# One gain row spread over the partitions by VectorE, and the normed rows of four tiles kept transposed in DRAM, in a hybrid decoder block on eight cores

## The reference, cut to what matters

```python
h = rms_norm(x, norm_mix_g)                  # the normed rows; norm_mix_g is "g1" below
proj = h @ w_in                              # (B, S, 5888)
a_b, a_c, a_v, q, k, v, g_a, g_b = split(proj)
y_a = (a_b * causal_dwconv(a_c * a_v)) @ w_proj_a
y_b = dilated_window_attention(q, k, v) @ w_proj_b      # windows 128, 512, 2048 at steps 1, 4, 16
x = x + (sigmoid(g_a + b0) * y_a + sigmoid(g_b + b1) * y_b) @ w_out
h = rms_norm(x, norm_ffn_g)
gate, val = split(causal_dwconv(h @ w_up))
x = x + (silu(gate) * val) @ w_down
return rms_norm(x, final_norm_g)
```

## Time and profile before

| | |
|---|---|
| Time, median of 3 runs | 1986.63 us |
| Profiled execution's own time | 1988.9 us |
| Its span, slowest core (core 4) | 1987.1 us |
| Spans of cores 0 to 7 | 1972.9, 1979.2, 1974.5, 1980.3, 1987.1, 1982.2, 1977.1, 1981.4 us |
| TensorE (PE) busy, core 4 | 1931.8 us, 97% |
| VectorE (DVE), ScalarE (ACT), GpSimd (POOL) busy | 57%, 42%, 33% |
| Mean DMA rate | 115 GB/s |

### The profile page before, as it was taken

One profiled execution on the slowest core, in us unless ns is written; L12 is line 12 of the kernel. 1 busy time (PEld: TensorE's weight loads), 2 busy tenths in 40 slices (PEclk: granted clock), 3 DMA queues, 4 the chain that ended last, 5 costly groups with the idle time before them and its releaser, 6 DMA issues.

```text
span 1987.1 us, 37890 instructions; the slowest of 8 cores (1972.9 to 1987.1 us)
## 1 busy us (share of the span) xinstructions
PE 1931.8 (97%) x11515; PEld 1020.8 (51%) x11662; DVE 1142.3 (57%) x1751; ACT 837.3 (42%) x1682; POOL 646.6 (33%) x1431
## 2 busy tenths in 40 slices
PE   6899999999999999999999999999999999999998
PEld 4666665655555444444445555655444444444443
DVE  3556663574444534535236576858684939577582
ACT  2456563552122212122224454736563727355361
POOL 1544420001112111020334254545453626354341
PEclk9999999999999999999999999999999999999999
DMA  9568997494538523524479923131322222221201
GB/s 182 175 151 207 235 209 149 107 185 111 157 102 180 150 58 113 167 42 131 69 194 189 166 80 82 47 114 43 122 67 79 73 85 70 67 88 33 85 1 53
DMA packets 196045, 229.49 MB, mean 115 GB/s; under 512 B 116916, under 2 KB 139322, under 8 KB 195464
## 3 DMA queue, kind: packets, MB, share of 16 engines
q1 hardware_dynamic: 178056, 192.86, 35.2%
q0 software_dynamic: 17792, 34.20, 11.4%
HBM read 161.90 MB, written 72.57 MB: 118 GB/s over the span
## 4 chain that ended last, share of the span: by engine, by line
PE 90%; DMA 4%; issue 2%; POOL 1%; ACT 1%; DVE 1%; SPq 0%; POOLq 0%; ACTq 0%; DVEq 0%
PE psp L684 63%; PE psp L1623 15%; PE psp L1350 6%; PE psp L690 3%; DMA v_d<-arena 1%; PE psp L582 1%; DMA arena<-w_in 1%; PE psp L553 1%; DMA arena<-x_loc 1%; PE psp L455 0%; DMA arena<-v_d 0%; POOL rstd L331 0%; DVE arena L1576 0%; ACT arena L556 0%; ACT arena L432 0%
## 5 line engine op out<-in xcount | busy, mean ns | idle before, releaser
L684 PE MATMUL psp<-arena 128*128 128x512 bf16 (+4 forms) x6741 | 1333.4, 357 | 10.8 <-DVE arena L265 2.7
L684 PEld LDWEIGHTS psp<-arena 128*128 128x128 bf16 x6848 | 661.8, 98 | 657.2 <-issue 12.0
L1576 DVE SCALAR_TENSOR_TENSOR arena<-psp,fcw_s,arena 128x511 f32<-128x511 f32 (+4 forms) x792 | 522.3, 687 | 81.8 <-ACT arena L1569 26.8
L1623 PE MATMUL psp<-arena 128*128 128x512 bf16 x1378 | 303.5, 379 | 1.6
L1569 ACT ACTIVATE arena<-psp,fcb_s,fcw_s 128x512 f32<-128x512 f32 (+1 forms) x396 | 286.1, 731 | 0.3 <-ACT uc L1567 0.2
L1591 POOL TENSOR_TENSOR arena<-arena 128x512 bf16<-128x512 bf16 (+1 forms) x198 | 218.6, 1104 | 72.2 <-ACT arena L1589 28.4
L432 ACT ACTIVATE arena<-arena 128x1024 bf16<-128x1024 f32 (+1 forms) x114 | 120.1, 1053 | 268.5 <-DVE arena L1648 251.6
L1623 PEld LDWEIGHTS psp<-arena 128*128 128x128 bf16 x1408 | 137.7, 98 | 166.2 <-issue 1.0
L1309 DVE TENSOR_TENSOR arena<-psp,arena 128x512 f32<-128x512 f32 (+2 forms) x144 | 90.3, 632 | 221.6 <-PE psp L684 217.1
L1295 ACT ACTIVATE arena<-psp,bg_s 128x512 f32<-128x512 f32 (+2 forms) x144 | 92.1, 640 | 272.2 <-PE psp L684 268.6
L1313 POOL TENSOR_TENSOR arena<-arena 128x512 bf16<-128x512 f32 (+2 forms) x72 | 82.6, 1147 | 277.1 <-DVE arena L1309 222.3
(11 more groups left out here) (88 smaller groups left out, 954.0 us busy)
## 6 DMA issues: line engine op xcount, KB each, us to landing
arena<-x_loc SPq DMA_DIRECT2D x80, 512.0 KB, 5.9
arena<-x_d SPq DMA_DIRECT2D x64, 512.0 KB, 3.7
h_d<-arena SPq DMA_DIRECT2D x65, 256.0 KB, 6.3
x_d<-arena SPq DMA_DIRECT2D x32, 512.0 KB, 5.0
out<-arena SPq DMA_DIRECT2D x32, 512.0 KB, 2.7
u_d<-arena SPq DMA_DIRECT2D x96, 132.0 KB, 6.0
arena<-u_d SPq DMA_DIRECT2D x32, 396.0 KB, 4.1
arena<-w_up POOLq DMA_DIRECT2D x22, 512.0 KB, 15.8
```

The lines of the kernel that those rows point to most:

```text
L684: S.add("pe", lambda e, kc=kc: e.matmul(out, lhsT=wap[:, kc, col0:col0 + 128], rhs=rhs(kc), start=(kc == 0), stop=(kc == kcn - 1), skip_gr ...
L1576: S.add("dve", lambda e, b=b, t=t, sh=sh, wv_=wv_, lo=lo: e.scalar_tensor_tensor(out=tmpC[t][:, lo:n], in0=ps[b][:, o + lo - sh:w_ - sh], ...
L1623: S.add("pe", lambda e: e.matmul(ps[b], lhsT=at[:, bi * 128:(bi + 1) * 128], rhs=wt[:, kk, hf * 512:(hf + 1) * 512], start=(k_ == 0), stop ...
```

## The change

There are two parts.

First, g1. A VectorE memset clears g1b, the DMA loads g1 into partitions 0, 32, 64 and 96 alone, and a VectorE stream shuffle copies, within each group of 32 partitions, the first partition to all. `scale_g` goes ahead of the first `stat`.

Second, the kept rows. The row-wise stores to h_d stay only for tiles 4 to 7. For tiles 0 to 3, the transposed slot hTA is stored as a whole (128 partitions of 8 KB, 1 MB) to a new tensor hT_d: tile 0 after `a_tile(-2)`, tiles 1, 2 and 3 after their own `a_tile`. The last four columns of tile -1 go to hh_d after `a_tile(-1)`. `hb_load` reads tiles 0 to 3 with plain loads of up to 512 columns, and tiles 4 to 7 with transposing loads as before. For piece 0 the four columns of hh_d are loaded first, and the next load writes the same key, so SP waits for the first to land before it issues the second.

```diff
+    hT_d = dscr("hT_d", [4, 128, KC, 512])
+    hh_d = dscr("hh_d", [128, KC, 4])
...
+    S.add("dve", lambda e: e.memset(g1b, 0.0), writes=[("g1b",)])
     for q in range(4):
         emit_xload()
         if q == 0:
-            cdma(g1b, g1_d.partition_broadcast(128), ("g1b",), newsem("s_g1b"))
+            cdma(g1b[0:128:32, :], g1_d.partition_broadcast(4), ("g1b",), newsem("s_g1b"))
+            S.add("dve", lambda e: e.stream_shuffle(g1b, g1b, [0] * 32), reads=[("g1b",)], writes=[("g1b",)])
...
-        if t != "E" and (t >= 0 or (t, b) == (-1, 3)):
+        if t != "E" and t >= 4:
             r0 = h_row(t, b)
             S.add("sp", lambda e: e.dma_start(out=h_d[r0:r0 + 128, :], in_=hb), reads=[hk], writes=[("h_d", t, b)],
...
-        for q in range((BW[j] + 127) // 128):
-            c0 = BS[j] + 128 * q
-            n = min(128, (BW[j] - 128 * q + 15) // 16 * 16)
-            blks = range((c0 - 4) // 128, (c0 + n - 5) // 128 + 1)
-            S.add("sp", lambda e: e.dma_start(out=hTB[i][:, :, 128 * q:128 * q + n], in_=h_d[2044 + c0:2044 + c0 + n, :],
-                                              transpose=True),
-                  reads=[("h_d", k // 4, k % 4) for k in blks], writes=[("hTB%d" % i, q)], dma_sem=sem_hb[i][q])
+        col = 0
+        if j == 0:
+            S.add("sp", lambda e: e.dma_start(out=hTB[i][:, :, 0:4], in_=hh_d[:, :, :]), reads=["hh_d"],
+                  writes=[("hTB%d" % i, 0)], dma_sem=sem_hb[i][3])
+            col = 4
+        while col < BW[j]:
+            k0 = BS[j] + col - 4
+            t, o = k0 // 512, k0 % 512
+            q = col // 128
+            if t < 4:
+                n = min(BW[j] - col, 512 - o)
+                S.add("sp", lambda e: e.dma_start(out=hTB[i][:, :, col:col + n], in_=hT_d[t, :, :, o:o + n]),
+                      reads=[("hT_d", t)], writes=[("hTB%d" % i, p) for p in range(q, (col + n + 127) // 128)],
+                      dma_sem=sem_hb[i][q])
+            else:
+                n = 128
+                S.add("sp", lambda e: e.dma_start(out=hTB[i][:, :, col:col + n], in_=h_d[2048 + k0:2048 + k0 + n, :],
+                                                  transpose=True),
+                      reads=[("h_d", t, o // 128)], writes=[("hTB%d" % i, q)], dma_sem=sem_hb[i][q])
+            col += n
...
     def start_norms():
 
+        scale_g(g1b, ("g1b",))
         stat(0)
-        scale_g(g1b, ("g1b",))
         start_loads(0)
...
     for t in SEQ:
         a_tile(t)
+        keep = {-2: 0, 1: 1, 2: 2, 3: 3}.get(t)
+        if keep is not None and keep < 4:
+            S.add("sp", lambda e: e.dma_start(out=hT_d[keep], in_=hTA[slot_of[keep]]), reads=hk(slot_of[keep]),
+                  writes=[("hT_d", keep)], dma_sem=newsem("s_hk%d" % keep))
+        if t == -1:
+            S.add("sp", lambda e: e.dma_start(out=hh_d[:, :, :], in_=hTA[slot_of[-1]][:, :, 508:512]), reads=hk(slot_of[-1]),
+                  writes=["hh_d"], dma_sem=newsem("s_hh"))
```

## The result

The changed kernel took 1998.02 us (median of 4 runs, 1995.97 to 2003.43) where the kernel before took 1986.85 beside it: a ratio of 1.006, 95% interval 1.004 to 1.0081. It is slower by some 11 us, and I had forecast 5.7 us faster; 1998.02 lies above the upper end of my range and above the rival with the lumps, 1991.2. The profiled execution took 1998.55 us; its slowest core is core 6 with a span of 1997.0, on which the kernel before took 1977.1. For one experiment, the store made three times, two of the four runs in its ratio of 1.0106 (1.0065 to 1.0148) were disturbed on one die, and its profiled run is read instead.

A forecast was written before the change was run, and what follows sets the result against it. PE was busy 1931.8 of 1987.1 us; the first 75 us were held bound by DMA, through x1, weights and x5. Start -7.0 plus later stores +1.3 gave -5.7 us: 1980.9 from a median of 1986.63, range 1976.5 to 1987.5.

The forecast's parts named there:

- the rival with the lumps: Tiles 1 to 3's 1 MB stores each delay loads and u_d stores by 3.9 us: 4.6 slower, 1991.2 us; chance 0.08.
- I take 6.5: At the start, without g1's broadcast, row block x1 lands at 6.5 us instead of 11.77, moving the weights' chain 5.3 us.
- the rival with x1 at 10.3: At the start, memset starts late, x1 to x3 stand behind g1 on SP: -1.9 us, 1984.7; inside the same 0.28.
- The other rival: Something else holds the weights' queue, so only PE's first start moves: -1.1 us, 1985.5; chance 0.28.
- signs of a wrong prediction: Third weight after 34 us, first multiply after 14, or PE newly losing over 4 us between 95 and 275 us.
- First multiply 12.5, first projection 22.4: At the start, first multiply at 12.5 us against 14.89, first projection at 22.4 against 24.77: PE starts 2.4 us earlier.
- 1.7 us between x4 and x5 by the h_d stores: In the early row loads, without tile 0's 256 KB store between them, x5 comes 1.7 us sooner.
- 15.3 us, which I hold fixed: Serial stretch behind x5, from POOL's roots of block 5 at 51.64 to PE going on at 66.95, taken as unchanged.
- Four of 1 MB and a small one: the same bytes: Four 1 MB stores and a small one replace 17 of 256 KB: same bytes, later, in lumps, same queue.
- 0 to 3 us late, I take 0: Tile 0's 1 MB store, issued near 103 us, is 0 to 3 us late for the slot's next user; priced at 0.
- Tiles 1 to 3, 1.3 us in sum: Tiles 1 and 2: nothing, or up to 3.9 us each; tile 3's store in full DMA from 250 us: 1.3 taken.
- `hb_load` at 0: In stage B, 17 transposing loads become plain; its 2.6 idle us of 625 bound the gain, taken as 0.

The follow-up runs named there:

- the pair on one chip: The changed kernel and the same with tile -1's four columns kept in SBUF, each against the kernel before on one chip: ratios 1.007 and 1.0006.
- the kernel with the columns: Changed kernel with tile -1's last four columns copied by POOL to SBUF and back, replacing the hh_d store and load: ratio 1.0009, in a second run 1.0006.

## Why the prediction was wrong

**"I take 6.5" for x1: mis-sized.** On core 4, of which the forecast spoke, x1 landed at 9.87 against 11.77, 1.9 sooner in place of 5.3; in the mean at 9.25 against 10.49, 1.2 sooner; on core 6 at 9.70, 0.7 later than before. The changed kernel's timeline, core 6:

```profile
1.35 0.91 DVE L390 MEMSET arena<- 128x1024 f32 x1 [1.35 <-PEq L135]
...
2.34 0.70 SPq L273 DMA_DIRECT2D arena<-g  x1
...
3.10 1.33 SPq L384 DMA_DIRECT2D arena<-x_loc  x3
...
5.32 1.29 DVE L395 STREAM_SHUFFLE arena<-arena 128x1024 f32<-128x1024 f32 x1
...
10.26 4.36 POOL L319 DMA_DIRECT2D arena<-w_in  x6 [7.89 <-DMA arena<-x_loc]
...
12.82 2.47 DVE L447 SCALAR_TENSOR_TENSOR arena<-arena,rstd 128x1024 bf16<-128x1024 f32 x2
...
22.50 2.77 PE L694 MATMUL psp<-arena 128*128 128x256 bf16 x13
```

and of the kernel before, x1's piece of the chain, then two rows of the timeline:

```profile
1.99 6.98 DMA arena<-x_loc
```

```profile
12.10 2.47 DVE L443 SCALAR_TENSOR_TENSOR arena<-arena,rstd 128x1024 bf16<-128x1024 f32 x2
...
21.83 5.43 PE L690 MATMUL psp<-arena 128*128 128x256 bf16 x34
```

I had seen that SP is held for the memset and reckoned an issue at 2.6 "while x0 is still landing" as harmless. It was 3.10 (1.99 before), x0 had landed at 4.91, and x1 took 6.6 us from its issue. With x1 issued ahead of g1 it lands at 7.6 to 7.7 in the mean: standing behind g1 and the memset costs 1.6. And the broadcast held less than I put down to it: with nothing between, x1 needs 2.6 us behind x0, where I took 1.5, so that of the 5.5 us between them in the mean 2.9 were there to win, and of core 4's 7.0 some 4.4. Taking the lower end from a count of bytes was the error; the rival with x1 at 10.3, behind g1 on SP, was nearer in number and in mechanism, though the memset didn't start late (1.35). The other rival, that the start is not bound by x1, is out: where x1 came 2.8 to 2.9 us sooner, the third weight came 3.2 to 3.4 sooner. Two of the signs of a wrong prediction came: the third weight landed after 34 (34.6 in the mean, 34.8 on core 4), and PE lost more than 4 us between 95 and 275 us.

**First multiply 12.5, first projection 22.4: near in number, partly by luck; the gain was smaller.** Core 6 has 12.82 and 22.50, but it had 12.10 and 21.83 before. On core 4 they went from 14.89 to 13.14 and from 24.77 to 23.19, 1.8 and 1.6 us in place of 2.4, and in the mean they gained 0.4 each. The shuffle took 1.29 us where I took 1.28. The Trainium skill's rate (VectorE: DVE Perf Modes, The perf-mode tier table), by which I had an estimate of 1.2, agrees.

**1.7 us between x4 and x5 by the h_d stores: right, and worth little.** x5 came 3.07 us behind x4 in place of 4.73 (means). What failed is "15.3 us, which I hold fixed": from x5's landing to tile -1's first keys it took 16.9 us before and 17.9 after (means), so two thirds of the 1.7 were lost again behind x5. POOL's roots, block by block from block 4 to block 8, the first line of a set each on core 6, in the kernel before (its fourth set left out):

```profile
43.24 0.24 POOL L333 TENSOR_SCALAR ssq<-ssq 128x1 f32<-128x1 f32 x1 [27.61 <-ACT arena L432]
...
48.08 0.22 POOL L333 TENSOR_SCALAR ssq<-ssq 128x1 f32<-128x1 f32 x1 [2.28 <-ACT arena L432]
...
50.84 0.22 POOL L333 TENSOR_SCALAR ssq<-ssq 128x1 f32<-128x1 f32 x1
...
58.14 1.08 POOL L333 TENSOR_SCALAR ssq<-ssq 128x1 f32<-128x1 f32 x1 [0.52 <-ACT arena L432]
```

and in the changed kernel:

```profile
46.61 0.24 POOL L335 TENSOR_SCALAR ssq<-ssq 128x1 f32<-128x1 f32 x1 [30.25 <-ACT arena L436]
...
50.14 0.50 POOL L335 TENSOR_SCALAR ssq<-ssq 128x1 f32<-128x1 f32 x1 [0.97 <-ACT arena L436]
...
53.18 1.25 POOL L335 TENSOR_SCALAR ssq<-ssq 128x1 f32<-128x1 f32 x1
...
56.96 1.25 POOL L335 TENSOR_SCALAR ssq<-ssq 128x1 f32<-128x1 f32 x1
...
60.61 0.22 POOL L335 TENSOR_SCALAR ssq<-ssq 128x1 f32<-128x1 f32 x1
```

Before, POOL waits 2.28 us for x5; after, 0.97, and then it runs without a break. From block 4 to block 8 it takes 14.9 us before and 14.0 after. By these rows, an x5 that comes sooner by more than 0.97 us would be late at POOL. The question "what is late next" I had asked for VectorE and for PE, not for POOL.

**"Four of 1 MB and a small one: the same bytes": the step that failed and decided.** The small one got no price of its own; by its bytes it was nothing. It cost 8.5 us at 108 to 118, and 10.8 up to 400 us in the pair on one chip (13.7 against 2.9). "0 to 3 us late, I take 0" for tile 0's store is right without the pieces (7.8 us to land, no wait). No row of before shows a store of pieces that small, so it should have had bounds from the nearest row instead of nothing. The Trainium skill (DMA: Bandwidth & Descriptors, Why small descriptors are slow (HBM only)) speaks of some three cycles a packet and 32 bytes of metadata for each DMA operation. By an estimate from that page, with each piece as one operation, 1024 x 40 bytes are 41 KB, 0.3 us at the 154 KB per us of the earlier trace rows; core 6's trace shows 5.2 us without any transfer, and the measurement decides.

**Tiles 1 to 3, 1.3 us in sum: too little.** The stores of tiles 2 and 3 cost an estimated 1 to 3 us (1 of shift, 2.8 of time, neither clear of the scatter); on the chip of the pair the kernel with the columns fell back by 3.1, and the loss there goes with the number of tiles kept, which points to these stores without showing it. Of the lumps rival the place and the mechanism were right (u_d buffers, the full DMA of rows 11), and its sign; but tile 0's store with the pieces ahead of it, not these, decided. `hb_load` at 0 was right: from 430 to 1100 us PE idles 1.0 us in the mean over the cores, 0.8 before.

The sum that was: -1.1 for the start, +8.5 for the stop, +5.3 behind it (an estimated 1 to 3 for the stores of tiles 2 and 3; the rest stays open). Without the small store the change comes out at 1.0006 to 1.0009 of the kernel before: the small store made it slower, and the start's small gain and the kept tiles' stores are why it would not have been faster either.

## What to carry to other kernels

Price a DMA by its pieces, not by its bytes, and look at what is in its queue ahead of it as well as behind: 8 KB in 1024 pieces stopped PE here about as long (8.5 us) as 1 MB stored three times (7.6). A store that reads a buffer in use turns any delay of its queue into a stop of the engine that writes the buffer next; a few columns of a row are better kept in SBUF or packed first. When a transfer on the path comes sooner, ask of each engine in the chain behind it how long its own list is, and look at the granted clock behind each stop; and don't put a load that waits for an engine ahead of loads that need not.

## What the runs showed of the hardware

- A store of 8 KB in 1024 pieces of 8 bytes, alone in the kernel before, lands after 8.9 to 16.1 us; behind it no transfer ran for 5.2 us on core 6 of the changed kernel, and a 1 MB store issued 0.5 us ahead of it is held too (17.4 us to land). In 128 pieces of 64 bytes the 8 KB land after 3.6 to 5.2 us.
- Tile 0 stored three times (3 MB) has landed 15.0 us after the first issue on core 6, some 200 KB per us; behind the pieces 1 MB alone took 14.8.
- The first step of a set of roots on POOL takes 1.25 us in place of 0.22 where it starts 0.12 us into a VectorE multiply of 1.28, and ends just behind it (53.18 beside 53.06 to 54.34, and 56.96 beside 56.84). Starting 0.05 us into one it took 0.22, and the multiply 1.31 (kernel before, 50.84 beside 50.79).
- Where PE idled 3.6 to 8.0 us from 100 to 125 us, the granted clock of that stretch was 0.80 to 0.87; in the kernel before, with 0 to 1.3 us, it was 1.00 on every core.
- A load of 16 KB issued by ScalarE at 2.33 us had landed only at 10.4, while SP's queue moved row blocks issued up to 2.44; issued by SP at 2.34, ahead of x1, it had landed by 5.3 (core 6).
